# Feeding the first up projection before its root is known: whole residual tiles and an unnormed first chunk in a two-block kernel

## The reference, cut to what matters

```
h = h + mix @ w_out                       # 1024 -> 1024, the "out" stage
xn = h * rsqrt(mean(h*h) + EPS) * norm_ffn_g
u = xn @ w_up                             # 1024 -> 5632, the "up" stage
u = causal convolution of width 3 over tokens, per column, + conv_b
a, g = split(u)
h = h + (silu(g) * a) @ w_down            # the "down" stage
```

## Time and profile before

| | us |
|---|---|
| median of 3 runs | 1170.05 |
| the profiled execution | 1169.52 |
| its span | 1167.8 |
| TensorE busy in it | 1161.3 (99%) |
| VectorE, ScalarE, GpSimd busy | 561.4, 515.9, 464.7 |

### The profile page before, as it was taken

The page is one execution under the profiler, slowest core; times in us unless marked ns, Lnnn a source line. Parts: engine busy times, 40 slices in busy tenths (PEclk is TensorE's granted clock), DMA queues, the critical chain, the costliest instruction groups (busy, mean ns, idle before and its releaser), DMA issues.

```text
span 1167.8 us, 16077 instructions
## 1 busy us (share of the span) xinstructions
PE 1161.3 (99%) x5934; PEld 953.4 (82%) x5934; DVE 561.4 (48%) x1123; ACT 515.9 (44%) x816; POOL 464.7 (40%) x189
## 2 busy tenths in 40 slices
PE   9999999999999999999999999999999999999999
PEld 7787778988888888888988676789888888888887
DVE  4364345977777774212574566726434433440000
ACT  5534653634443432322545577835443444331110
POOL 6542314434434433444443314043443443434442
PEclk9999999999999999999999999999999999999999
DMA  8322222554554543223332110122223223212222
GB/s 309 111 90 91 67 79 79 210 199 170 207 209 168 198 158 87 97 99 111 132 121 104 54 38 1 38 72 102 82 106 108 78 102 108 89 58 98 99 99 97
DMA packets 27859, 132.08 MB, mean 113 GB/s; under 512 B 3488, under 2 KB 5152, under 8 KB 18976
## 3 DMA queue, kind: packets, MB, share of 16 engines
q1 hardware_dynamic: 25920, 128.90, 31.2%
q10 hardware_dynamic: 1888, 2.49, 0.7%
HBM read 129.28 MB, written 2.10 MB: 112 GB/s over the span
## 4 chain that ended last, share of the span: by engine, by line
PE 98%; ACT 2%; issue 0%; DVE 0%; POOL 0%; ACTq 0%; POOLq 0%
PE psum L1607 87%; PE psum L1688 2%; PE psum L1676 2%; PE psum L2146 1%; PE psum L1848 1%; PE psum L1951 1%; ACT prob L748 1%; ACT probT L731 1%; PE psum L1830 0%; PE psum L2052 0%; PE psum L1916 0%; PE psum L2089 0%; PE psum L1646 0%; PE psum L2074 0%; PE psum L1954 0%
## 5 line engine op out<-in xcount | busy, mean ns | idle before, releaser
L493 POOL TENSOR_TENSOR wl<-raw,wh 128x2048 fp32r<-128x2048 f32 (+1 forms) x88 | 364.4, 4141 | 497.8 <-ACT wh L663 285.0
L1607 PE MATMUL psum<-xh,wh 128*128 128x512 f32 (+1 forms) x1008 | 382.9, 380 | 0.0
L1607 PE MATMUL psum<-xh,wl 128*128 128x512 f32 (+1 forms) x1008 | 378.6, 376 | 0.0
L1607 PE MATMUL psum<-xl,wh 128*128 128x512 f32 (+1 forms) x1008 | 378.6, 376 | 0.0
L1254 DVE SCALAR_TENSOR_TENSOR scratch<-psum,cols,scratch 128x511 f32<-128x511 f32 (+1 forms) x176 | 131.7, 748 | 196.3 <-ACT scratch L809 188.3
L1607 PEld LDWEIGHTS psum<-xh,wh 128*128 128x128 f32 x1008 | 189.6, 188 | 39.0 <-issue 3.5
L1607 PEld LDWEIGHTS psum<-xh,wl 128*128 128x128 f32 x1008 | 189.7, 188 | 34.6
L1607 PEld LDWEIGHTS psum<-xl,wh 128*128 128x128 f32 x1008 | 189.7, 188 | 33.8 <-issue 0.2
L663 ACT ACTIVATE wh<-raw 128x2048 fp32r<-128x2048 f32 (+1 forms) x50 | 88.4, 1768 | 243.8 <-PE psum L1607 243.8
L1607 PE MATMUL psum<-acth,wh 128*128 128x512 f32 (+2 forms) x378 | 141.8, 375 | 0.0
L1607 PE MATMUL psum<-acth,wl 128*128 128x512 f32 (+2 forms) x378 | 141.7, 375 | 0.0
(11 more groups left out here) (273 smaller groups left out, 1383.9 us busy)
## 6 DMA issues: line engine op xcount, KB each, us to landing
raw<-stream SPq DMA_DIRECT2D x69, 1024.0 KB, 4.7
ada_raw<-ada SPq DMA_DIRECT2D x48, 512.0 KB, 5.5
raw<-down SPq DMA_DIRECT2D x32, 704.0 KB, 4.0
gains_and_h<-xT SPq DMA_DIRECT2D x7, 256.0 KB, 5.7
raw<-stream SPq DMA_DIRECT2D x7, 256.0 KB, 6.0
outT<-gains_and_h SPq DMA_DIRECT2D x7, 256.0 KB, 5.2
rel<-rel_tiles ACTq DMA_DIRECT2D x1, 1344.0 KB, 8.1
wsT<-w_spatial_T SPq DMA_DIRECT2D x1, 512.0 KB, 5.9
```

The costliest lines, as they stand in the source:

```text
L493: pool.tensor_tensor(wl[slot][:, 0:w], raw[slot][:, 0:w], wh[slot][:, 0:w].bitcast(F32), ALU.subtract).then_inc(lo_done, 1)
L1607: ins = pe.matmul(out, lhs[a], rhs[b], start=first and n == 0, stop=last and n == 2)
```

## The change

The second block keeps the old form; the first gets its own functions. In the out stage tiles 6 and 7 become whole tiles of 512 columns. After each pair of residual tiles ScalarE also rounds h * ffn_g to `raw_high`, and VectorE makes `raw_low` from it; TensorE makes the first up pair (banks 0 and 1) from these, without the root. The sum over features becomes one matmul of 512 columns, ahead of k = 3 of that pair. ScalarE then makes the root twice, in PSUM (`WHOLE_ROOT`) and in SBUF (`ss_acc`). VectorE multiplies banks 0 and 1 by the SBUF root, and makes the normed tiles whole, 512 columns, from the PSUM root, for the second pair and all later chunks. The rounding of the chunk `up + 1` moves ahead of the root, that of `up + 2` into the normed tiles in quarters. Two `ada_sum`s move behind `conv(0)` and `conv(1)`.

```diff
+            raw_high = sb("raw_high", [P, KD, T], F32R, s)   # in the room of v1, q1, k1, decays
+            raw_low = sb("raw_low", [P, KD, T], F32R, s)
+        RAW_EXIT = KD - 3
+        WHOLE_TILES = bank[4:6]
+        WHOLE_ROOT = bank[6]
+        LAST_SQUARES = OUT_BANKS[(KD - 1) % 4]
+        def raw_square_room(m):
+            return SQUARES if m < KD - 1 else LAST_SQUARES
...
             low_edge(BASE1["up"] + 1, 0)
-            lows(BASE1["up"] + 2, N1)
+            low_edge(BASE1["up"] + 2, 3)
+            lows(BASE1["up"] + 3, N1)
...
# ScalarE
+            def raw_out(res, norm, base):
+                for c in range(KD // 2):
+                    for m in (2 * c, 2 * c + 1):
+                        square(norm, m, res.h, m + 1, m + 1, room=raw_square_room(m))
+                    if c < KD // 2 - 1:
+                        split_next(base + c, res.mm, 2 * c + 2)
+                    for m in (2 * c, 2 * c + 1):
+                        act.activation(raw_high[:, m, :], h[:, m, :], ACT.Copy, scale=col("ffn_g", m)).then_inc(norm.hi, 1)
+            def whole_high(norm, res, L, base):
+                n = base + KD // 2
+                for x in range(4):
+                    split_quarter(n - 1, x, res.mm, KD, True)
+                act.wait_ge(norm.ss, 1)
+                act.activation(ss_acc[:, :], WHOLE_ROOT[:, :], ACT.Ln, bias=eps_c[:, :], scale=1.0 / D).then_inc(norm.rstd, 1)
+                act.wait_ge(norm.rstd, 1)
+                act.activation(WHOLE_ROOT[:, :], ss_acc[:, :], ACT.Exp, scale=-0.5).then_inc(norm.rstd, 1)
+                act.activation(ss_acc[:, :], ss_acc[:, :], ACT.Exp, scale=-0.5).then_inc(norm.rstd, 1)
+                for k in range(KD):
+                    act.wait_ge(norm.tmp, k + 1 if k < RAW_EXIT else k + 3)
+                    act.activation(xh[:, k, :], WHOLE_TILES[k % 2][:, :], ACT.Copy).then_inc(norm.hi, 1)
+                    if k == RAW_EXIT - 1:
+                        for r in range(2):
+                            act.wait_ge(norm.tmp, RAW_EXIT + r + 1)
+                            first_tap(L, r, r)
+                    if 3 <= k < KD - 1:
+                        split_quarter(n, k - 3, L.mm, 2, True)
...
# VectorE
+            def raw_out(res, norm):
+                zero(norm, ss_acc)
+                for m in range(KD):
+                    if m in (0, 4):
+                        ada_sum(m // 2 + 2)
+                        ada_sum(m // 2 + 3)
+                    if m == 4:
+                        for e in range(2):
+                            dve.tensor_copy(CSIL_HALVES[e][:, :], csil[:, T * e:T * e + T]).then_inc(csil_moved, 1)
+                    add_residual(res, m, (FIRST_OUT[m] if m < 2 else OUT_BANKS[m % 4]), m + 1, None)
+                    add_square(norm, ss_acc, m, room=raw_square_room(m))
+                    if m % 2:
+                        for k in (m - 1, m):
+                            dve.wait_ge(norm.hi, k + 1)
+                            dve.scalar_tensor_tensor(raw_low[:, k, :], h[:, k, :], col("ffn_g", k), raw_high[:, k, :].bitcast(F32),
+                                                     ALU.mult, ALU.subtract).then_inc(norm.lo, 1)
+            def whole_tiles(norm, L):
+                dve.wait_ge(norm.rstd, 2)
+                for x in range(KD + 1):
+                    if x < KD:
+                        if x >= 2:
+                            dve.wait_ge(norm.lo, KD + x - 1)
+                        dve.scalar_tensor_tensor(WHOLE_TILES[x % 2][:, :], h[:, x, :], col("ffn_g", x), WHOLE_ROOT[:, :], ALU.mult, ALU.mult).then_inc(norm.tmp, 1)
+                    if x:
+                        dve.wait_ge(norm.hi, KD + x)
+                        dve.tensor_tensor(xl[:, x - 1, :], WHOLE_TILES[(x - 1) % 2][:, :], xh[:, x - 1, :].bitcast(F32), ALU.subtract).then_inc(norm.lo, 1)
+                    if x == RAW_EXIT - 1:
+                        dve.wait_ge(norm.rstd, 3)
+                        for r in range(2):
+                            dve.wait_ge(L.mm, r + 1)
+                            dve.tensor_tensor(bank[r][:, :], bank[r][:, :], ss_acc[:, :], ALU.mult).then_inc(norm.tmp, 1)
...
+                    late = 2 * (ADA_EARLY in ada_tiles)
-                    for x in ada_tiles[0:2]:
+                    for x in ada_tiles[0:2 - late]:
                         ada_sum(x)
                     conv(0)
                     conv(1)
-                    for x in ada_tiles[2:4]:
+                    for x in ada_tiles[2 - late:4]:
                         ada_sum(x)
...
# TensorE
-                for m in range(2, WHOLE):
+                for m in range(2, KD if a == 0 else WHOLE):
...
+                if a == 0:
+                    return
...
+            def pair_by_features(banks, slot, mm, norm, low0, features, aside=None, at=None):
+                for k in range(KD):
+                    if k == at:
+                        aside()
+                    pe.wait_ge(norm.lo, low0 + k + 1)
+                    for e in range(2):
+                        a = PAIR_COLS * k + P * e
+                        ins = split_product(banks[e][:, :], weights(slot, a, a + P), features(k), k == 0, k == KD - 1)
+                        if k == KD - 1:
+                            ins.then_inc(mm, 1)
+            def raw_and_first_pair(L, norm, base):
+                def raw_features(k):
+                    return raw_high[:, k, :], raw_low[:, k, :]
+                def whole_sum():
+                    pe.wait_ge(norm.acc, KD + 1)
+                    pe.matmul(WHOLE_ROOT[:, :], ones[:, :], ss_acc[:, :], start=True, stop=True).then_inc(norm.ss, 1)
+                pe.wait_ge(lo_done, base + 1)
+                pe.wait_ge(norm.acc, KD)
+                pair_by_features(bank[0:2], base % 2, L.mm, norm, 0, raw_features, whole_sum, 3)
+                pe.wait_ge(lo_done, base + 2)
+                pair_by_features(bank[2:4], (base + 1) % 2, L.mm, norm, KD, inputs)
```

More of the change, by code:

```diff
@@ L149, in build @@
             actl = sb("actl", [P, KF, T], F32R, s)
+        with ExitStack() as s:
+            raw_high = sb("raw_high", [P, KD, T], F32R, s)
+            raw_low = sb("raw_low", [P, KD, T], F32R, s)
         with ExitStack() as s:
@@ L581, in _ @@
                 if x == 0:
-                    pool.wait_ge(hi_edge, 4)
+                    pool.wait_ge(hi_edge, 7)
                 else:
@@ L586, in _ @@
                     (lo_first, lo_done)[x], 1)
-            low_edge(base, 4, True)
-            low_edge(base + 1, 7)
+            low_edge(base, 7, True)
+            low_edge(base + 1, 10)
             pool.wait_ge(res_down1.h, KD + 1)
@@ L642, in _ @@
             lows(BASE2["out"] + 2, BASE2["up"] + 1)
-            low_edge(BASE2["up"] + 1, 10)
+            low_edge(BASE2["up"] + 1, 13)
             lows(BASE2["up"] + 2, BASE2["down"])
@@ L687, in quarters, with first_tap @@
                 return {tile: lambda x=x: split_quarter(n, x, used, value, True) for x, tile in enumerate(tiles)}
+            def raw_out(res, norm, base):
[24 more added lines that the diff above has]
+                        split_quarter(n, k - 3, L.mm, 2, True)
+            def first_tap(L, r, tile):
+                act.activation(scratch[r][:, :], bank[r][:, :], ACT.Identity, bias=col(L.b, tile),
+                               scale=col(L.w, 3 * tile + 2)).then_inc(L.base, 1)
             def square(norm, m, ready, value, added, tokens=slice(0, T), room=SQUARES):
@@ L801, in residual_down, with up @@
                     square(norm, KD - 1, res.h, KD, KD, half(0), DOWN_PIECES[0])
-            def up(L, base):
+            def up(L, base, raw_norm=None):
                 act.preload_act_table(ACT.Silu)
@@ L807, in start @@
                     def start(r):
+                        if first and raw_norm is not None and r < 2:
+                            return
                         act.wait_ge(L.mm, i * 4 + (r + 1))
@@ L812, in four_tiles @@
                     start(0)
-                    split_next(base, L.mm, i * 4 + 2, i_landed)
+                    if not first or raw_norm is None:
+                        split_next(base, L.mm, i * 4 + 2, i_landed)
                     start(1)
@@ L927, in _ @@
             attend(0, prob1, probT1, neg_max1, row_sum1, 0, beside)
-            residual_out(res_out1, norm_ffn, BASE1["out"])
-            norm_high(norm_ffn, eps_c, None, after_out(res_out1, norm_ffn, BASE1["out"]))
-            up(up1, BASE1["up"])
+            raw_out(res_out1, norm_ffn, BASE1["out"])
+            whole_high(norm_ffn, res_out1, up1, BASE1["out"])
+            up(up1, BASE1["up"], norm_ffn)
             def cosines():
@@ L1187, in after_out @@
                         4: lambda: piece_residual(res, gain, 3), 5: lambda: piece_square(norm, 3)}
-            def residual_out(res, norm, gain, ada_too):
+            def raw_out(res, norm):
[14 more added lines that the diff above has]
```

(19 more changed lines are left out.)

## The result

The changed kernel takes 1176.82 us (median of 6 runs, 1176.21 to 1178.24), the kernel before 1169.82 (6 runs, 1169.80 to 1170.07). The ratio is 1.006, 95% interval 1.005 to 1.007: 7.0 us slower. The prediction was 1177.4 us, range 1173.5 to 1180.0. The profiled execution is at 1176.52 us with a span of 1174.8, 7.0 more than before. Since lines were added above them, the functions have new numbers: `split_product` is now L1689 (L1607 before), the residual L1224, the square sum L1195, and the new `raw_low` is L1256.

What follows compares the result with a forecast made beforehand. The prediction took TensorE's own instruction stream as the bound (busy 1161.3 of 1167.8 us). Its terms, -1.25 + 6.2 + 2.4 = +7.35 us on a median of 1170.05, gave 1177.4 us, range 1173.5 to 1180.0.

Steps and rivals of the forecast that it cites:

- Term 1: TensorE, tiles 6 and 7 and first up pair: half matmuls become whole ones, one whole sum; -1.25 us.
- Term 2: Out stage: VectorE's raw_low stands behind running GpSimd subtractions, delaying residuals and chunks; TensorE stands at the raw pair, +6.2 us.
- Term 3: TensorE after the pause of 6 us: its clock has fallen and matmuls run slowly at first; +2.4 us.
- Terms at nothing: From the raw pair's start on: root, normed tiles, later chunks and moved ada_sums come in time; no cost.
- A: Rival in the out stage: raw_low does not stand behind GpSimd, only the whole-tile gain is left; 1168.8 us, chance 0.10.
- B: Rival at the raw pair: TensorE stalls but its clock does not fall; 1175.0 us, chance 0.17.
- C: Rival: one block fewer, for instance at pair 2, 2.9 us of stall; 1171.7 to 1174 us, chance 0.06.
- D: Rival: more on top, a longer slow clock or conv(2) late by 1 to 1.5 us; 1179 to 1182, chance 0.10.

Runs made afterwards that it cites:

- e2_low_moved: The changed kernel with VectorE's raw_low moved in its list, behind the square sums of tiles 2, 5, 6 and 7: 1168.48 us, ratio to before 0.999.
- e6_halves: e2_low_moved with its raw pair made in token halves again, 96 matmuls of 256 columns for 48 of 512: 1169.26 us.
- e3_psum_input: The changed kernel with one operand of the eight raw_low taken from PSUM (bank 7) instead of raw_high, low part wrong: 1168.34 us, ratio to before 0.999.
- e1_high_first: The changed kernel with ScalarE's two raw_high put in front of split_next, the chunk's rounding: 1169.10 us, ratio to before 0.9996.
- e4_kept_busy: The changed kernel with 26 unread matmuls of 512 columns into bank 2 in front of the raw pair's waits: 1174.71 us, ratio to before 1.0044.
- e7_sums_back: e2_low_moved with the two ada sums back in front of conv(0): 1169.15 us, ratio to before 0.9997.
- e5_last_pair: The changed kernel with only pair 2's two raw_low moved, behind tile 6's square sum: 1172.89 us, ratio to before 1.0025.

## Why the prediction was right, point by point

- **Term 1 (-1.25 us).** Right. `e2_low_moved` is 1.1 us faster than before (its interval reaches from nearly nothing to 2.2), and its span is 1.1 less (1166.7 against 1167.8). By its trace the stretch itself is 1.23 shorter. `e6_halves` puts back one half of the half matmuls and 0.6 to 0.8 us.
- **Term 2 (+6.2 us).** Right in place, order and size: 6.07. The residuals of tiles 2, 4 and 6 were forecast at 182.94, 197.35 and 208.38 and stand at 182.97, 197.35 and 208.26; GpSimd's chunks at 188.20 and 202.61 and stand at 188.22 and 202.59. `e3_psum_input` shows the cause, as it leaves list, waits and lengths and changes one operand's place: GpSimd runs, one input is in PSUM, and nothing stands. `e1_high_first` shows the other condition: both inputs are in SBUF, GpSimd rests, and nothing stands. The mean of `raw_low` is 2.2 us, where the prediction said near 2.5. The Trainium skill ("SBUF — State Buffer", section "SBUF: two separate sides") calls it a lock that the first comer keeps; the traces agree where GpSimd is first (4.6 us for the first `raw_low` of a pair, `ada_sum` 5.09 in `e1_high_first`), and no run here shows VectorE first with GpSimd held up by it.
- **Term 3 (+2.4 us).** Right in kind, 0.3 to 0.5 too much: 2.1 us by the profile after (13.86 - 11.74), 1.9 to 2.1 by `e4_kept_busy`. The price was taken from the kernel's start, 20 passes at twice their time; here it was ten matmuls of 512 columns, eight of them 0.2 longer each. That the one price was near the other is in part luck, as the prediction named the two cases different. The Trainium skill's statement ("TensorE: Matmul & The Clock Gate", Part 1), a fall to 1.2 GHz when idle and a return after sustained work, agrees with this trace: the granted clock is 0.50 when TensorE begins again, and the matmuls are slow for about 4 us.
- **Terms at nothing.** They held. The chunk of tiles 6 and 7 came in time, the normed tiles too. The moved `ada_sum`s were the closest: in the profile after, conv(2) begins at 244.32 and takes 1.5, and VectorE had also to wait 2.2 us for the reloaded tile, which the count put under GpSimd's chunk. With the second pair from 224.33, TensorE wants bank 2 at 224.33 + 10.88 + 10.88 = 246.1. It ends at 245.9 and so has 0.2 to spare. In `e2_low_moved`, without the clock's loss, conv(2) starts at 236.25 and ends at 237.8, its bank is wanted at 204.48 + 33.5 = 238.0, and there is no wait either. The prediction had counted a tie here and taken nothing; that it came out at nothing, by 0.2 us in both, is luck. `e7_sums_back` shows that a count this close can be wrong by 0.3.
- **The sum.** With the measured terms, -1.23 + 6.07 + 2.1 = +6.9, against 7.0 measured and 7.35 forecast. The number is right because the terms are, and not by errors that cancel.
- **The rivals.** A (1168.8) is what `e3_psum_input` and `e2_low_moved` measure, 1168.3 and 1168.5, but not this change. B (1175.0) is `e4_kept_busy`, 1174.7. C (1171.7 to 1174) is `e5_last_pair`, 1172.9: the same stall as in C, though made by moving `raw_low` in the list. D did not come.

## What to carry to other kernels

An instruction that is new in the middle of an engine's list costs what stands behind it, and its own length may be the smallest part: check where its operands lie, and what GpSimd does at that moment. Here the same instructions make the kernel 7 us slower or 1 us faster than before, by where three pairs of them stand in one list. In a kernel whose TensorE is 99% busy, price a pause as its length and the clock's return behind it: a third more for the 6.07 us here, half as much again for the 2.8 us of `e5_last_pair`.

## What the runs showed that was not expected

Behind a pause of 2.8 us the clock had fallen in six of eight executions of `e5_last_pair`, and not in the other two, which are 1.2 and 1.6 us below the median of the six. Only the profiled one of the six has a trace; its windows (columns as above) show the level:

```profile
204.80:207.50 2.70, 0.13 (x1) 0.00 (x0) 2.70 (x2) 0.00 (x0) 2.70 (x1) 0.90 0.00 0
207.60:209.00 1.40, 1.40 (x3) 1.13 (x4) 1.40 (x3) 0.00 (x0) 0.00 (x0) 0.50 0.28 35
```

Why two executions kept the clock no run here shows. Behind the pause the matmuls were 0.427 apart for 2.7 us, behind the pause of 6.07 for 4.0; the kernel's start, from which the price was taken, has 4.6 us at its slow rate.
